# Hybrid decoder layer: input parts on two queues, a third unit in split precision, x's rows loaded later

## The reference, cut to what matters

```python
def reference(x, mem, ...):
    x = x + hybrid_mixer(x, mem, ...)
    x = x + moe_ffn(rms_norm(x, norm_ffn_g), ...)
    return x

def hybrid_mixer(x, ...):
    h = rms_norm(x, norm_mix_g)
    proj = h @ w_in
    q_sb, k_sb, v_sb, x_rg, gate_rg, q_ca = jnp.split(proj, IN_SPLITS, axis=-1)
    ...
```

## Time and profile before

| | |
|---|---|
| median of 3 runs | 588.15 us (587.84 to 588.36) |
| profiled execution | 588.95 us, of which the span is 587.2 us |
| TensorE busy | 552.8 us, 94% of the span |
| VectorE, ScalarE busy | 208.9 us (36%), 159.2 us (27%) |
| loads | 225.90 MB read, 386 GB/s over the span |

### The profile page before, as it was taken

The page is one execution under the profiler, slowest core; times in us unless marked ns, Lnnn a source line. Parts: engine busy times, 40 slices in busy tenths (PEclk is TensorE's granted clock), DMA queues, the critical chain, the costliest instruction groups (busy, mean ns, idle before and its releaser), DMA issues.

```text
span 587.2 us, 8291 instructions
## 1 busy us (share of the span) xinstructions
PE 552.8 (94%) x3148; PEld 305.7 (52%) x3149; DVE 208.9 (36%) x532; ACT 159.2 (27%) x307; POOL 24.3 (4%) x78
## 2 busy tenths in 40 slices
PE   8999999999999999999999999999969999289994
PEld 6988875465544445555344554555534455034441
DVE  2879789664335222220122222222221222102212
ACT  5786376242212112220021222222221211101112
POOL 1005240000000000000000000000000000000000
PEclk9999999999999999999999999999998999679999
DMA  8997559659999999999999999999999999999993
GB/s 318 418 419 289 214 204 424 253 222 350 424 395 419 423 421 420 427 427 423 426 423 426 426 419 430 431 423 423 424 429 426 431 420 436 428 411 410 417 408 142
DMA packets 26776, 227.50 MB, mean 387 GB/s; under 512 B 3184, under 2 KB 3312, under 8 KB 7664
## 3 DMA queue, kind: packets, MB, share of 16 engines
q1 hardware_dynamic: 26592, 226.93, 93.2%
q10 hardware_dynamic: 144, 0.03, 0.0%
HBM read 225.90 MB, written 1.05 MB: 386 GB/s over the span
## 4 chain that ended last, share of the span: by engine, by line
PE 79%; DMA 14%; DVE 4%; issue 1%; ACT 1%; SPq 0%; DVEq 0%; ACTq 0%
PE ps L1760 30%; PE ps L1789 13%; DMA cell_three<-in_w_e 9%; PE ps L1719 8%; PE ps L1799 7%; DMA cell_two<-in_w_e 5%; PE ps L1624 5%; PE ps L1520 4%; PE ps L1487 3%; PE ps L1501 2%; PE ps L1780 1%; PE ps L1509 1%; DMA wA<-in_w_qk 1%; PE ps L1766 1%; PE ps L1772 1%
## 5 line engine op out<-in xcount | busy, mean ns | idle before, releaser
L1760 PE MATMUL ps<-cell_two,xg 128*64 128x512 f32 (+2 forms) x496 | 110.0, 612 | 18.6 <-DMA cell_three<-in_w_e 14.0
L1789 PE MATMUL ps<-cell_d,e_hT 128*64 128x512 f32 (+2 forms) x440 | 87.6, 597 | 2.2 <-DVE e_hT L1383 1.5
L1760 PE MATMUL ps<-cell_gu,xg 128*64 128x512 f32 (+2 forms) x416 | 78.3, 594 | 0.0
L1380 DVE TENSOR_TENSOR e_h<-e_sg,ps 128x256 f32<-128x256 f32 x28 | 11.8, 421 | 186.2 <-ACT e_sg L897 186.2
L1760 PEld LDWEIGHTS ps<-cell_two,xg 128*64 128x64 f32 (+2 forms) x496 | 34.5, 132 | 82.6 <-issue 82.6
L897 ACT ACTIVATE e_sg<-ps 128x256 f32<-128x256 f32 x28 | 10.8, 384 | 208.5 <-PE ps L1760 208.5
L1438 DVE SCALAR_TENSOR_TENSOR ylo<-ps,gslot,yhi 128x512 fp32r<-128x512 f32 x52 | 39.0, 750 | 72.0 <-ACT yhi L908 72.0
L1719 PE MATMUL ps<-pick,xhi 128*128 128x256 f32 x224 | 58.5, 300 | 0.3 <-DVE pick L1296 0.3
L908 ACT ACTIVATE yhi<-ps,gslot 128x512 fp32r<-128x512 f32 x52 | 35.7, 687 | 69.4 <-PE ps L1789 69.3
L1719 PE MATMUL ps<-pick,xlo 128*128 128x256 f32 x224 | 54.3, 281 | 0.0
L1719 PEld LDWEIGHTS ps<-pick,xhi 128*128 128x128 f32 x224 | 42.2, 188 | 19.1 <-issue 18.8
(11 more groups left out here) (336 smaller groups left out, 674.7 us busy)
## 6 DMA issues: line engine op xcount, KB each, us to landing
cell_two<-in_w_e SPq DMA_DIRECT2D x31, 2048.0 KB, 25.8
cell_d<-in_w_e SPq DMA_DIRECT2D x51, 1024.0 KB, 22.1
cell_gu<-in_w_e SPq DMA_DIRECT2D x48, 1024.0 KB, 15.0
cell_three<-in_w_e SPq DMA_DIRECT2D x9, 3072.0 KB, 23.0
wo<-in_w_out SPq DMA_DIRECT2D x1, 4096.0 KB, 12.3
wA<-in_w_qk SPq DMA_DIRECT2D x7, 512.0 KB, 10.8
wR<-in_w_rest SPq DMA_DIRECT2D x3, 1024.0 KB, 28.6
wV<-in_w_v SPq DMA_DIRECT2D x1, 2048.0 KB, 18.8
```

The source lines that it names most:

```text
L1380: nc.vector.tensor_tensor(dst[:].rearrange("q k p -> q (k p)"), e_sg[:], ps[:, U, DE:2 * DE], ALU.mult).then_inc(sem, 1)
L1760: last = mm(ps[side * w:(side + 1) * w, U, :], rows(k, slice(side * w, (side + 1) * w)), weight[:, k - k0, :], start=k == 0, stop=k == KD - 1)
L1789: last = mm(ps[side * w:(side + 1) * w, Y[half], :], e_hT[:, kk, side * w:(side + 1) * w], n[:, kk, half * 512:(half + 1) * 512], start=kk ...
```

## The change

x_t and the first weight block come in three parts (slices 0 and 1, 2 and 3, 4 to 7) in place of two halves. The parts of x_t stay on SP's queue; those of the block go to ScalarE's queue, behind `vec`. The slices are dealt alternately to VectorE (even) and ScalarE (odd). SP issues x's rows behind wA[3] in place of wA[1]. Unit 2 becomes split like units 3 to 7; its high part takes a new place at `o_more`, an expert cell, so SP waits for unit 2 before it loads the first expert there. Unit 2 first runs all products with the high weight, then waits for the low one. The norm becomes a walk item, behind the splits of units 2 and 3 and ahead of that of unit 4; the broadcast row is issued within unit 3, behind its fourth slice. The semaphore of the router's biases is merged into that of its weights.

```diff
-    hi_at = [r.offset - 4 * KB, r.offset, o_ring + 56 * KB, o_ring + 60 * KB, o_ring + 88 * KB]
+    hi_at = [r.offset - 4 * KB, r.offset, o_ring + 56 * KB, o_ring + 60 * KB, o_ring + 88 * KB, o_more]
...
-        walk = [("split_u", 3), ("split_u", 4), ("unit", 0), ("unit", 1), ("unit", 2), ("row", 0), ("split_u", 5), ("unit", 3),
+        walk = [("split_u", 2), ("split_u", 3), ("norm", 0), ("split_u", 4), ("row", 0), ("unit", 0), ("unit", 1), ("unit", 2),
+                ("split_u", 5), ("unit", 3),
                 ("split_u", 6), ("unit", 4), ("split_u", 7), ("log1p", 0), ("split_w", 0), ("unit", 5),
...
-        ACT_K, DVE_K = [0, 1, 4, 5], [2, 3, 6, 7]
+        ACT_K, DVE_K = [1, 3, 5, 7], [0, 2, 4, 6]
+        PART_OF = [0, 0, 1, 1, 2, 2, 2, 2]
...
         def _(sp):
-            for i in range(2):
-                c = slice(i * KD // 2, (i + 1) * KD // 2)
-                sp.dma_start(xT_in[:, c], x_t[:, c]).then_inc(xT_half[i], 16)
-                sp.dma_start(wA[0][:, c], w_qk[0, :, c]).then_inc(wA0_half[i], 16)
+            for i in range(3):
+                c = slice(PART_OF.index(i), PART_OF.index(i) + PART_OF.count(i))
+                sp.dma_start(xT_in[:, c], x_t[:, c]).then_inc(xT_part[i], 16)
             for n in range(1, 8):
                 sp.dma_start(wA[n][:], w_qk[n]).then_inc(wA_loaded[n], 16)
-                if n == 1:
+                if n == 3:
                     sp.dma_start(x_in[:], x[0].rearrange("(t p) d -> p t d", p=P)).then_inc(x_loaded, 16)
...
+            sp.wait_ge(unit_ps, 3)
             load_fixed("low", 1)
...
-            sp.dma_start(rbias[:], router_bias[0].partition_broadcast(P)).then_inc(rb_loaded, 16)
+            sp.dma_start(rbias[:], router_bias[0].partition_broadcast(P)).then_inc(rt_loaded, 16)
...
             act.dma_start(vec[:], vec_t).then_inc(vec_loaded, 16)
+            for i in range(3):
+                c = slice(PART_OF.index(i), PART_OF.index(i) + PART_OF.count(i))
+                act.dma_start(wA[0][:, c], w_qk[0, :, c]).then_inc(wA0_part[i], 16)
...
             split_a(0)
-            act.wait_ge(x_loaded, 16)
-            squares(x_in, 0, 0)
-            root(0, 1)
...
+                elif kind == "norm":
+                    act.wait_ge(x_loaded, 16)
+                    squares(x_in, 0, 0)
+                    root(0, 1)
...
+                elif kind == "norm":
+                    mean_eps(0, 2)
+                    inverse(0, 1)
+                    dve.wait_ge(xn_dve, 2)
+                    dve.wait_ge(consts, 2)
+                    for t in range(NT):
+                        nc.vector.tensor_scalar(rstd_diag[:, t, :], ident[:], stat[:, 2 + t:3 + t], None, ALU.mult).then_inc(diag_dve, 1)
...
+                    if n == 2:
+                        pe.wait_ge(whi_act, split_count("split_u", n))
+                    else:
+                        pe.wait_ge(wlo_dve, split_count("split_u", n))
                     pe.wait_ge(alo_dve, 1)
                     w, w_hi, w_lo = split_of(n)
-                    for k in range(KD):
+                    if n == 2:
+                        for k in range(KD):
+                            for m, a in enumerate((hT_hi, hT_lo)):
+                                mm(b[:, 0:SEQ], w_hi[:, k, :], a[:, k, :], start=k == 0 and m == 0, stop=False)
+                        pe.wait_ge(wlo_dve, split_count("split_u", n))
+                        for k in range(KD):
+                            last = mm(b[:, 0:SEQ], w_lo[:, k, :], hT_hi[:, k, :], start=False, stop=k == KD - 1)
+                    for k in range(KD if n > 2 else 0):
+                        if n == 3 and k == 4:
+                            broadcast_row()
```

More of the change, by code:

```diff
@@ L322, in hybrid_decoder_layer @@
             memT_loaded, x_loaded, mem_loaded, vec_loaded, wg_loaded, wV_loaded, kv_loaded, wo_loaded, x1_loaded,
-            rt_loaded, rb_loaded, consts, zeroed, ssq_act, std_act, xn_dve, diag_dve, row_ps, row_act,
+            rt_loaded, consts, zeroed, ssq_act, std_act, xn_dve, diag_dve, row_ps, row_act,
             xT_act, xT_dve, unit_ps, unit_act, unit_dve, conv_dve, z_ps,
@@ L334, in hybrid_decoder_layer @@
         ) = [ctx.enter_context(nc.semaphore(name)) for name in """
-            memT_loaded x_loaded mem_loaded vec_loaded wg_loaded wV_loaded kv_loaded wo_loaded x1_loaded             rt_loaded rb_loaded consts zeroed ssq_act std_act xn_dve diag_dve row_ps row_act xT_act xT_dve
+            memT_loaded x_loaded mem_loaded vec_loaded wg_loaded wV_loaded kv_loaded wo_loaded x1_loaded             rt_loaded consts zeroed ssq_act std_act xn_dve diag_dve row_ps row_act xT_act xT_dve
             unit_ps unit_act unit_dve conv_dve z_ps bc_act mask_pool w_dve
@@ L344, in hybrid_decoder_layer @@
         """.split()]
-        xT_half = [ctx.enter_context(nc.semaphore(f"xT_half{i}")) for i in range(2)]
-        wA0_half = [ctx.enter_context(nc.semaphore(f"wA0_half{i}")) for i in range(2)]
-        wA_loaded = [ctx.enter_context(nc.semaphore(f"wA_loaded{n}")) for n in range(8)]
+        xT_part = [ctx.enter_context(nc.semaphore(f"xT_part{i}")) for i in range(3)]
+        wA0_part = [ctx.enter_context(nc.semaphore(f"wA0_part{i}")) for i in range(3)]
+        wA_loaded = [None] + [ctx.enter_context(nc.semaphore(f"wA_loaded{n}")) for n in range(1, 8)]
         wR_loaded = [ctx.enter_context(nc.semaphore(f"wR_loaded{g}")) for g in range(3)]
@@ L377, in hybrid_decoder_layer @@
         rg_cols = {14: (0, 0), 15: (0, P), 16: (1, 0), 17: (1, P)}
-        hi_place = {3: 0, 4: 1, 5: 2, 6: 3, 7: 0, 14: 2, 15: 3, 16: 0, 17: 4}
+        hi_place = {2: 5, 3: 0, 4: 1, 5: 2, 6: 3, 7: 0, 14: 2, 15: 3, 16: 0, 17: 4}
         hi_left = {7: 3, 14: 5, 15: 6, 16: 7, 17: 11}
@@ L715, in _ @@
             for k in ACT_K:
-                act.wait_ge(xT_half[k // (KD // 2)], 16)
+                act.wait_ge(xT_part[PART_OF[k]], 16)
                 nc.scalar.mul(hT[:, k, :], xT_in[:, k, :], vec[:, MIX + k:MIX + k + 1]).then_inc(xT_act, 1)
@@ L964, in _ @@
             for k in DVE_K:
-                dve.wait_ge(xT_half[k // (KD // 2)], 16)
+                dve.wait_ge(xT_part[PART_OF[k]], 16)
                 nc.vector.tensor_scalar(hT[:, k, :], xT_in[:, k, :], vec[:, MIX + k:MIX + k + 1], None,
@@ L1040, in _ @@
             split_a(0)
[L1041 to L1046, removed]
             def conv(c):
@@ L1268, in _ @@
             evac_x2T(1, 0)
-            dve.wait_ge(rb_loaded, 16)
+            dve.wait_ge(rt_loaded, 32)
             dve.wait_ge(consts, 3)
@@ L1474, in _, with broadcast_row @@
                 mm(ps[:, 0, 0:SEQ], ident[:], zeros[:], start=True, stop=True)
+            def broadcast_row():
+                pe.wait_ge(diag_dve, NT)
+                for t in range(NT):
+                    last = mm(ps[:, 4, t * P:(t + 1) * P], ones[:], rstd_diag[:, t, :], start=True, stop=True)
+                last.then_inc(row_ps, 1)
             def unit(n):
@@ L1494, in unit @@
                         if n == 0:
-                            pe.wait_ge(wA0_half[k // (KD // 2)], 16)
+                            pe.wait_ge(wA0_part[PART_OF[k]], 16)
                             if k in ACT_K:
@@ L1559, in _ @@
                     unit(n)
[L1560 to L1564, removed]
                 elif kind == "z" and n % 2 == 0:
@@ L1675, in _ @@
             project(10)
-            pe.wait_ge(rt_loaded, 16)
+            pe.wait_ge(rt_loaded, 32)
             router(0, 0)
```

1 line of the change is left out of this document (removed).

## The result

The changed kernel takes **590.72 us** (median of 10, 590.07 to 593.85) against 588.26 us for the kernel before (10 runs beside it): a ratio of 1.0041, with a 95% interval of 1.0029 to 1.0053. The forecast was 588.05 us, within 587.3 to 588.9. The change costs 2.5 us, and the step of the prediction that failed is the one on the three parts and the two queues.

What follows compares the result with a forecast made beforehand. The expert-weight stream was taken as the bound, its start set by routing and unit 8. Unit 4's evacuation at 23.18 us against 23.28 gains 0.10 us: 588.15 - 0.10 = 588.05 us, range 587.3 to 588.9.

Steps and rivals of the forecast that it cites:

- the three parts and the two queues: Front loads: block 0 from ScalarE's queue becomes usable between 8.25 and 9.5 us; the middle, 8.9 us, was taken.
- X: Landing of x's rows, when ScalarE's first square starts: 12.05 us before, forecast 14.56 us, 2.51 us later.
- X + 8.54: First moment VectorE can evacuate unit 4, counted from the landing of x's rows: 23.10 us.
- K: Moment the last part of weight block 0 is usable in unit 0: 8.22 us before, forecast 8.9 us.
- K + 14.25: End of unit 4 on TensorE, counted from block 0's last part becoming usable: 23.15 us.
- VectorE's path: VectorE's casts, subtractions and evacuations behind x's rows, up to unit 4's evacuation: X + 8.54, 23.10 us.
- the sum: Unit 4's evacuation at 23.18 us against 23.28 before, the later of two engine paths: 0.10 us gained.
- TensorE's path: Units 0 to 4 and the broadcast row on TensorE: K + 14.25, 23.15 us, and no sooner than X + 8.34.
- rule of equal turns: DMA engines take one packet from each queue in turn, putting 1.26 us more ahead of block 0's last part.
- The rival: The faster front, against which the prediction itself set rows half as long in more packets.
- The slower rival: Block 0's last part comes late in unit 0, K 9.51 us: 0.5 us lost, 588.65 us, chance 0.28.
- The faster front: Two queues fill the slow start of the stream by 0.5 us: 0.68 us gained, 587.47 us, chance 0.22.

Runs made afterwards that it cites:

- the halves run: Changed kernel with x_t and block 0 in two halves on SP's queue, rest of the change kept: 588.06 us, 0.9994 of the kernel before.
- the last run: Changed kernel on one queue, x_t in halves with whole block 0 between them, five warm-up products: 588.73 us, 0.9998 of the kernel before.
- whole: Changed kernel with x_t and block 0 each in one load on SP's queue: 588.85 us with four warm-up products, 588.42 us with five.
- x_t cut: Against the halves run, the first half of x_t cut into two loads, block 0 still in halves: 589.80 us, 1.0020 of the kernel before.
- block cut: Against the halves run, the first half of block 0 cut into two loads, x_t still in halves: 589.39 us, 1.0019 of the kernel before.

## Why the prediction was wrong

*What held.* That unit 8 decides, and that the stream moves with it: unit 4's evacuation, unit 8 and the first routed load moved by 3.03, 3.05 and 3.04 us. The two paths: X + 8.54 was met to 0.02 us with thirds on one queue, and K + 14.25, with 0.98 for the clock, gives 26.21 us in the changed kernel, whose unit 4 ended at 26.30. The price of next to nothing for the third split unit and the later norm together: the halves run has them alone and comes out 0.12 us ahead at unit 8, by VectorE's path; its agreement with the 0.10 us of the sum, which TensorE's path with K at 8.9 us set, is luck.

*What failed* is the part "Three parts and two queues", in three ways.

Its bounds for K, 8.25 to 9.5 us, moved only the order of the bytes and took the rate of the front from the halves of before; K was 10.98. Each of the two edits alone passes the upper bound: the second queue with halves gives 9.84 us, 1.62 us late and not far from the 1.26 us of the rule of equal turns; thirds on one queue, loads of 128 and 256 KB in rows of 1 and 2 KB, give 10.56 us, 2.34 us late. Together they are 2.76 us late, less than the sum of the two, so the runs do not say how much of it belongs to which. The rival named it, "rows half as long in more packets", and gave it no price.

X was taken as 14.56 us by the bytes ahead of it. It came 1.41 us later. This alone, by X + 8.54, would have put unit 4's evacuation at 24.51 us, 1.2 us late. The change both moves x's rows back by the 2.5 us that were priced and slows what is ahead of them.

The clock was left out of the sum. It is 0.98 us of the changed kernel's profiled execution, whose clock fell at 9.30 us; with TensorE kept at work the 12 products took 0.86 us less, and the medians differ by 0.52 us. The trace of before could price a product at the lower clock: its four warm-up products took 3.78 us, 0.95 each, where one of unit 0 takes 0.44. The slower rival stopped at the wait and put 0.5 us on what cost 2.5.

*Point by point.* The late part, the slower rival, was the right mechanism with K mis-sized by 1.5 us and the clock missing; the chance of 0.09 for slower by over 0.2% was too small, since a new wait in unit 0 had no upper bound in the trace of before. Its sign came: TensorE's weight loads idled 0.81 us for the last part, over the 0.7 us that was named. The faster front had it backwards: with smaller parts the first products could start sooner (5.80 us on one queue), but the whole landed later.

*What stays open.* Why small loads slow the front this much. Rows alone do not say it: thirds on one queue are 2.47 us late at X against halves, of which the lower rates until 12.05 us (187 against 240, then 398 against 419 GB/s) explain (53 x 8.2 + 21 x 3.85) / 415 = 1.24 us. The other half is not in the mean rate, and the last run has a better rate than halves and a later X. Nor is the issuing ruled out on one queue: each load more pushes SP's later issues back by 0.42 us or more, x's rows are issued at 3.44 us (whole), 4.39 (halves), 5.03 (x_t cut) and 5.50 us (block cut), and land 10.0 to 10.4 us behind that in all four. No run moved the issues alone. It does not explain the changed kernel, whose rows of x are issued at 4.15 us, sooner than in halves, and land 11.8 us later. Which of the 16 DMA engines is last at each landing is open too.

## What to carry to other kernels

At the start of a kernel, a first load that is cut finer can start the work sooner and end it later: price its last part by what else is in flight, in turns, and let the whole front be slower in one of your rivals; here halves in rows of 2 and 4 KB did better than thirds and no worse than whole loads, and a second queue put the needed bytes behind unneeded ones. When a change adds a wait on TensorE behind its warm-up, price the clock with it, and look at more than one execution before a gain is put down to a longer warm-up: whether four products had raised the clock differed between profiled executions. Before moving a load back past others, sum both paths that follow from its landing; VectorE's held to 0.02 us, and it is only as good as the landing put into it.

## What the runs showed of the hardware

A full clock in the column is no proof of one: it reads 1.00 until the list of the granted clock begins, while the records of products start 0.43 us apart, and 0.22 us apart from the list's first entry on. In the changed kernel the clock was at full from 5.88 us and at 0.50 from 9.30 us, behind idle stretches of 1.35 and 0.56 us with 1.13 us of work between them; in the kernel with whole loads and five warm-up products it was at full from 5.63 us and stayed there over 0.87 us of idling.

By the Trainium skill (TensorE: Matmul & The Clock Gate, section Part 1: The HAM clock gate) the point at which the clock changes shifts from run to run. The traces agree: the kernel before and the one with the delay ahead of unit 8 are the same up to there, and the clock was at full from 6.51 us in one and from 7.16 us in the other; with the same four warm-up products it was at full from between 5.88 and 14.13 us in the profiled executions.

The rule of turns, one packet from each queue (the Trainium skill, DMA: Bandwidth & Descriptors, section Queues, rings and completion order), agrees with two landings that fall together: in the changed kernel the last 256 KB of block 0, by its shape 24 rows for each of 16 engines behind the 8 of the gains, landed at 10.98 us, and block 1, with 24 rows of x_t for each engine ahead of its own 8, not ahead of 10.8 us (2.18 plus at least 8.6 us).
